# A hybrid gMLP and retention layer on eight cores: two small transposing DMAs per retention step, and four gate groups held in PSUM

## The reference, cut to what matters

```
q = rotary(r_q);  k = rotary(r_k)                 # 8 heads, 128 wide
ret = retention(q, k, r_v)                        # per head, chunk by chunk of 128 tokens:
#   scores = (q k^T * decay);  out = scores v + (q R) * cross_decay
#   R = R * chunk_decay + (k * w)^T v             # the state, carried to the next chunk
#   out = standardize(out)                        # over the 256 values of a head
yb = (ret * silu(r_z)) @ w_ob                     # the gate, then a projection
out = (sigmoid(g_a + b) * ya + sigmoid(g_b + b) * yb) @ w_out
x = layer_norm(ALPHA * x + out)
```

## Time and profile before

| | us |
|---|---|
| median of three runs | 2732.95 (2732.89 to 2733.12) |
| the profiled execution, its own time | 2732.09 |
| its span on the slowest core (core 2) | 2730.5 |
| span of the even cores | 2728.6 to 2730.5 |
| span of the odd cores | 2684.2 to 2694.5 |
| PE busy / PEld / DVE / ACT / POOL on core 2 | 2697.4 / 1420.4 / 1108.5 / 643.5 / 194.5 |

### The profile page before, as it was taken

One profiled execution on the slowest core, in us unless ns is written; L12 is line 12 of the kernel. 1 busy time (PEld: TensorE's weight loads), 2 busy tenths in 40 slices (PEclk: granted clock), 3 DMA queues, 4 the chain that ended last, 5 costly groups with the idle time before them and its releaser, 6 DMA issues.

```text
span 2730.5 us, 42159 instructions; the slowest of 8 cores (2684.2 to 2730.5 us)
## 1 busy us (share of the span) xinstructions
PE 2697.4 (99%) x15129; PEld 1420.4 (52%) x15170; DVE 1108.5 (41%) x2686; ACT 643.5 (24%) x1546; POOL 194.5 (7%) x370
## 2 busy tenths in 40 slices
PE   8999999999999999999999999999999999999998
PEld 6556666555555666666544444444555444444443
DVE  1444441166664422222474343411666642122157
ACT  1221110155554111111001211111555621111100
POOL 2000000000000000000001000000000000000000
PEclk9999999999999999999999999999999999999999
DMA  9843444333225433344649464444333544444443
GB/s 159 175 78 63 69 74 71 60 63 58 47 53 109 70 73 68 69 70 70 143 174 214 81 93 72 73 87 76 63 63 63 108 78 89 74 70 86 77 122 134
DMA packets 62420, 241.54 MB, mean 88 GB/s; under 512 B 7424, under 2 KB 7552, under 8 KB 58624
## 3 DMA queue, kind: packets, MB, share of 16 engines
q0 software_dynamic: 52560, 193.49, 41.3%
q1 hardware_dynamic: 9648, 45.27, 4.6%
HBM read 413.31 MB, written 18.87 MB: 158 GB/s over the span
## 4 chain that ended last, share of the span: by engine, by line
PE 97%; DMA 1%; ACT 1%; issue 0%; DVE 0%; POOL 0%; POOLq 0%; DVEq 0%; ACTq 0%
PE ps_all L236 96%; PE ps_all L245 1%; DMA ring<-w 1%; ACT L257 0%; DVE xy_85 L264 0%; ACT aT L257 0%; POOL xT L292 0%; POOL ring L292 0%; POOLq L988 0%; ACT zth_124 L257 0%; DVE stv L282 0%; ACT rs_66 L257 0%; ACT rs_63 L257 0%; ACT rs_65 L257 0%; ACT zth_123 L257 0%
## 5 line engine op out<-in xcount | busy, mean ns | idle before, releaser
L236 PE MATMUL ps_all<-xT,ring 128*128 128x384 bf16 (+1 forms) x6400 | 1206.6, 348 | 0.8 <-ACT rs_65 L257 0.7
L236 PEld LDWEIGHTS ps_all<-xT,ring 128*128 128x128 bf16 x6400 | 622.1, 98 | 536.6 <-issue 2.4
L236 PE MATMUL ps_all<-ring,xT 128*128 128x512 bf16 (+1 forms) x3744 | 731.1, 353 | 5.1 <-DMA xT<-xT 3.1
L236 PEld LDWEIGHTS ps_all<-ring,xT 128*128 128x128 bf16 x3744 | 337.4, 98 | 341.1 <-issue 6.9
L236 PE MATMUL ps_all<-aT,ring 128*128 128x384 bf16 (+1 forms) x2520 | 481.2, 347 | 2.1
L236 PEld LDWEIGHTS ps_all<-aT,ring 128*128 128x128 bf16 x2560 | 250.2, 98 | 220.0
L292 POOL DMA_DIRECT2D ring<-w x352 | 187.7, 541 | 2409.9 <-PE ps_all L236 2013.4
L236 PE MATMUL ps_all<-ring,yT 128*128 128x512 bf16 x1088 | 235.2, 379 | 0.0
L236 PEld LDWEIGHTS ps_all<-ring,yT 128*128 128x128 bf16 x1088 | 106.4, 98 | 128.4
L275 DVE CAST yT<-ps_all 128x384 bf16<-128x384 f32 (+1 forms) x40 | 24.5, 611 | 205.7 <-PE ps_all L236 205.7
L264 DVE SCALAR_TENSOR_TENSOR ogb_129<-ogb_129,ps_all 128x384 f32<-128x384 f32 (+1 forms) x40 | 24.3, 608 | 183.6 <-PE ps_all L236 183.6
(11 more groups left out here) (271 smaller groups left out, 1895.4 us busy)
## 6 DMA issues: line engine op xcount, KB each, us to landing
ring<-w POOLq DMA_DIRECT2D x352, 512.0 KB, 6.3
xy_86<-x SPq DMA_DIRECT2D x9, 1024.0 KB, 6.8
out<-xy_86 SPq DMA_DIRECT2D x18, 512.0 KB, 3.1
xy_85<-x SPq DMA_DIRECT2D x8, 1024.0 KB, 5.4
out<-xy_85 SPq DMA_DIRECT2D x16, 512.0 KB, 2.6
xT<-xT POOLq DMA_DIRECT2D x9, 512.0 KB, 26.3
xT<-xT POOLq DMA_DIRECT2D x4, 1024.0 KB, 21.3
bias_71<-bias_s SPq DMA_DIRECT2D x2, 1024.0 KB, 12.2
```

The source lines that it names most:

```text
L236: return self.S.op("pe", lambda e: e.matmul(out, lhsT=l, rhs=r, start=start, stop=stop), [l, r], [out])
```

## The change: what it does

The two PE transposes of `ybp` and ACT's copy of their result go. In their place, right after the norm of a step has been written to `ybp`, SP issues two transposing DMAs of 128 x 128 bf16 each, from `ybp` straight into `aT`, with one key per half and buffer (eight keys). The state product moves from bank 4 to bank 7. Behind the loop, four gate groups instead of seven carry the rest of the retention steps (i = N to N+3); their results stay in banks 0 to 3 while the steps run; then comes one more `small_post`, and then the four tanh and their products. All later groups are gated at once, and take the banks in turn from bank 4. The area for the temporary buffers is 2 KB per partition larger, and the gate's and the prefix state's buffers begin 2 KB later in it.

```
+    def dma_tr(self, key, out, in_):
+        self.S.op("sp", lambda e: e.dma_start_transpose(out=out, in_=in_), [in_], [out], key=key)
...
         def small_pe(i):
-            a, b_, c_, y = i - 2, i - 3, i - 4, i - 7
+            a, b_, c_ = i - 2, i - 3, i - 4
...
-                    self.mm(self.bank(4)[:, 128:384], m.qkt[c_ % 6][:, 1, :], m.v[c_ % 6][:], True, True)
+                    self.mm(self.bank(7)[:, 0:256], m.qkt[c_ % 6][:, 1, :], m.v[c_ % 6][:], True, True)
...
-            if 0 <= y < N:
-                for j in range(2):
-                    self.tr(self.bank16(7)[:, j * 128:(j + 1) * 128], m.ybp[y % 4][:, j * 128:(j + 1) * 128])
...
         def small_post(i):
...
-                    self.stt(m.U[:, h, :], m.U[:, h, :], float(self.gC[h]), self.bank(4)[:, 128:384], ALU.mult, ALU.add)
+                    self.stt(m.U[:, h, :], m.U[:, h, :], float(self.gC[h]), self.bank(7)[:, 0:256], ALU.mult, ALU.add)
...
             if 0 <= z < N:
+                h, c = divmod(z, n)
                 self.act(m.ybp[z % 4][:], self.bank(5 + z % 2)[:, 0:256], AF.Identity, scale=r[:, 0:1], bias=r[:, 1:2])
-            if 0 <= y < N:
-                h, c = divmod(y, n)
-                self.act(self.aT[:, 2 * h:2 * h + 2, c * 128:(c + 1) * 128],
-                         self.bank16(7)[:, 0:256].rearrange("p (j t) -> p j t", j=2), AF.Copy)
+                for j in range(2):
+                    self.dma_tr("ty%d%d" % (j, z % 4), self.aT[:, 2 * h + j, c * 128:(c + 1) * 128], m.ybp[z % 4][:, j * 128:(j + 1) * 128])
...
+        def gate(ct, c0, k, b):
+            tk = slice(c0 * CH, (c0 + k) * CH)
+            ps = self.bank(b)[:, 0:k * CH]
+            th = m.zth[self.rot("zt", 4)][:, 0:k * CH]
+            self.act(th, ps, AF.Tanh, scale=0.5)
+            self.stt(th, th, 1.0, ps, ALU.add, ALU.mult)
+            a = self.aT[:, ct, tk]
+            self.stt(a, a, 0.5, th, ALU.mult, ALU.mult)
+
         i = N
-        step = 0
+        held = []
+        self.nbank = 4
         for ct in range(16):
             s = self.w_take(1)
             for (c0, k) in self.sp:
-                tk = slice(c0 * CH, (c0 + k) * CH)
-                drain = i < N + 7
-                b = step % 3 if step < 7 + 3 else self.next_bank()
-                step += 1
-                ps = self.bank(b)[:, 0:k * CH]
-                self.group(ps, [(m.ring[:, s, kt, :], self.xm(kt, c0, k)) for kt in range(KT)])
-                if drain:
+                b = i - N if i < N + 4 else self.next_bank()
+                self.group(self.bank(b)[:, 0:k * CH], [(m.ring[:, s, kt, :], self.xm(kt, c0, k)) for kt in range(KT)])
+                if i < N + 4:
+                    held.append((ct, c0, k, b))
                     small_pe(i)
                     small_post(i)
                     i += 1
-                th = m.zth[self.rot("zt", 4)][:, 0:k * CH]
-                self.act(th, ps, AF.Tanh, scale=0.5)
-                self.stt(th, th, 1.0, ps, ALU.add, ALU.mult)
-                a = self.aT[:, ct, tk]
-                self.stt(a, a, 0.5, th, ALU.mult, ALU.mult)
+                    if i == N + 4:
+                        small_post(i)
+                        for g in held:
+                            gate(*g)
+                else:
+                    gate(ct, c0, k, b)
             self.w_free()
```

More of the change, by code:

```diff
@@ L674, in small_pe @@
                 self.mm(ob, m.qkT[c_ % 4][:, 0, :], m.Rg[c_ % 3][:], False, True)
-            if 0 <= y < N:
-                for j in range(2):
-                    self.tr(self.bank16(7)[:, j * 128:(j + 1) * 128], m.ybp[y % 4][:, j * 128:(j + 1) * 128])
         def small_post(i):
-            a, b_, c_, y = i - 2, i - 3, i - 4, i - 7
-            z = i - 5
+            a, b_, c_, z = i - 2, i - 3, i - 4, i - 5
             if 0 <= z < N:
@@ L873, in plan_memory @@
     s0 = top[0]
-    top[0] += 32768
+    top[0] += 34816
     assert top[0] <= nc.sbuf_usable_end, (top[0], nc.sbuf_usable_end)
@@ L885, in sub @@
             pos[0] += (size + 31) // 32 * 32
-            assert pos[0] <= s0 + 32768
+            assert pos[0] <= s0 + 34816
             return at(name, shape, dt, off)
@@ L916, in plan_memory @@
     m.cs = a("cs", [128, NMAX, 128], F32)
-    assert a.pos[0] <= s0 + 24576
-    a = area(24576)
+    assert a.pos[0] <= s0 + 26624
+    a = area(26624)
     m.zth = [a("zth%d" % i, [128, 512], F32) for i in range(4)]
-    a = area(24576)
+    a = area(26624)
     m.yh = [a("yh%d" % i, [128, KT, 128], BF16) for i in range(2)]
```

## The result

The changed kernel takes 2712.03 us, against 2733.03 for the kernel before on the same chip: a ratio of 0.9922, 95% interval 0.9900 to 0.9945. Times are medians of all executions; ratios, and ranges of single executions (2711.18 to 2712.23 here), leave out those that ran slower at a lower clock on one die or both, which would move a median by 0.3 us at most, in e5 by 2.5. The gain is 21.0 us; 25.8 were forecast.

What follows compares the result with a forecast made beforehand. The prediction took PE, 97% of the slowest core's chain, as the bound. Its terms 13.3 + 9.5 + 3.0 = 25.8 us gave 2707 us; the forecast's own range was 2703 to 2712, the whole range 2702 to 2722.

Steps and rivals of the forecast that it cites:

- one term that was put at nothing: Waiting caused by the transposing DMAs that replace the PE transposes: forecast to add zero to the time.
- The two PE transposes: Retention loop: removing them saves PE 0.11 us per step over 122 steps, 13.3 us after one not gained.
- The drain: Last retention steps among the first gate groups: held gates gain 9.5 us in the first tile, 3.0 in the second.
- Is anything late next? ... Cost: nothing: Drain: bank 0 is free at 835.5, wanted at 840.7, 5 us to spare, so no new wait.
- The two DMAs: Per retention step, issued by SP: a pair gets through within 3.95 us, four buffers absorb lag; cost zero.
- I take zero: Cost forecast for the transposing DMAs; 5.38 us per pair was kept for the range.
- one pair of lag: Inside a weight burst at 5.38 us per pair, 2.7 pairs pass while 3.7 are made; four buffers cover it.
- The prediction's signs: Right: 3.95 us steps, seven groups in about 20 us, full clock, landing below 15 us. Wrong: ACT idle on DMAs.
- A: Rival: transposing DMAs set the loop's pace at 5.38 us per step, +149 us, 2882 us; chance 0.11.
- The mild form of A: Rival: DMA pair just above the loop step, 4.1 to 4.2 us paid in series, about 2731 us; chance 0.02.
- B: Rival: drain stays long as four held gates and last norms come in one lump, 2719.6; 0.07 together with C.
- C: Rival: loop step stays 4.06 us through the norm-DMA chain or DVE, only drain gains, 2720.5; 0.07 together with B.

Runs made afterwards that it cites:

- e5: Changed kernel with each transposing DMA cut in two, four of 64 x 128 per step; 2881.04 us, ratio 1.0527.
- e1: Changed kernel with eight ybp buffers and sixteen DMA keys instead of four and eight; 2706.29 us, ratio 0.9901.
- e2b: Changed kernel with the last head's weight refill moved later and made to wait for the tile's last transposing DMAs; 2707.32 us, ratio 0.9903.
- e7: Changed kernel with the transposing DMAs left out, so the normed output never reaches aT; 2707.0 us, ratio 0.9904.
- e6: Changed kernel with one transposing DMA of 128 x 256 per step instead of two of 128 x 128; 2712.34 us, ratio 0.9925.
- e2: Changed kernel with the weight refill put behind the drain in program order only, without a wait; 2710.38 us, ratio 0.9917.

## Why the prediction was right, and where it was not

The direction, the mechanism of both gains and the range held. The time lies at the upper end of the forecast's own range (2703 to 2712), 5 us above the 2707, and the reason is one term that was put at nothing. By its own steps:

**1. The two PE transposes: right.** 13.3 us forecast. Core 2 gained 818.16 - 810.73 = 7.43 in the first loop. From the first reader of `aT` to the second tile's first gate group it took 2159.74 - 959.53 = 1200.21 and takes 2140.53 - 946.76 = 1193.77, 6.44 less. Together 13.9. The 0.69 us in front of the second gate stayed (0.65), as the step said, though it did not grow.

**2. The drain: the second tile right (3.0 forecast and measured), the first tile mis-sized.** 9.5 us were forecast; the change gave 5.3 on core 2 and 1.7 on core 0. The layout itself was good: e1 runs the seven groups in 19.9 us, and one table load follows the last norm where they alternated before. What failed is the sentence "Is anything late next? ... Cost: nothing". It followed bank 0, which has time to spare, and passed over banks 5 and 6. The second and third group behind the held ones take these two, and the last two norms must have read them first. With the norms in time that costs nothing (e1); a late norm goes to PE there at once.

**3. The two DMAs: the pace right, the lag wrong, and this is the cause.** "I take zero" held in the loop: a pair takes SP 2.3 us of 3.95. It rested on one pair of lag "against four buffers", 15.8 us. The lag was too small even there: during a head's refill a DMA landed as late as 11.8 us (core 0, 700 to 795), three steps and not one, so the loop was covered with less to spare than forecast. And 15.8 us is the loop's reuse distance only. In the first tile's drain the change itself brings the steps closer, since a gate group lasts 2.60 us and a projection group 3.45, and the distance is 9.6 us (e1). At this very place the last head's four slots are refilled. There, on core 0, the DMA took 14.64 us, ACT's norm waited 6.89, PE 4.60, and the granted clock fell behind it. The term put at zero measures 137.88 - 131.70 = 6.2 us on core 0 and 136.03 - 131.70 = 4.3 on core 2. The second tile's groups last 3.45 us and its first steps keep 3.95; there one norm waits 1.78 us and PE does not, though its weights are refilled alike. The price taken from the earlier trace rows, 2.69 us per DMA one behind the other, was a wrong picture as well: issue costs 1.16 us each, and a DMA inside a burst is late by its landing, 14.64 us for the one that PE waited for, not by its spacing.

So the sum: 13.9 + 5.3 + 3.0 = 22.2 us on core 2, whose span fell from 2730.5 to 2708.3. Core 0, 0.9 us shorter before, is now longer by 2.3: its wait is the longer one, and its drain had less to gain (below). Where the wait is taken away the forecast's gain of 25.8 us is met, each against the kernel before on its chip: 27.0 (e1), 26.4 (e2b), 26.3 (e7).

The prediction's signs were the right ones to look for. Of those that would show it wrong, one appeared: idle time of ACT before a norm that ends with a DMA into `aT`. And of those that would show it right, three failed in the first tile's drain on core 0: the seven groups did not take about 20 us (the seventh began 832.00 - 809.94 = 22.1 us after the first), the granted clock did not stay full, and landing passed 15 us (19.4 at most).

**The rivals.** *A* did not happen with two DMAs per step and did with four (e5). The 1309 ns that the Trainium skill gives for a DMA transpose ("VectorE: DVE Perf Modes", The three transpose paths) made an estimated 2.6 us per pair; the rows show 2 x 1.16 = 2.3 to issue them, and e5 and e6 that this price is per DMA, not per size. Its advice for TensorE did not hold here: by the earlier trace rows against the loop above, two transposes cost PE's path 0.11 us per step and in the loop the DMAs cost it none. The mild form of A, each DMA paid behind the other, did not happen (e2b). The 2.0 us that the prediction takes for it from the Trainium skill ("DMA: Bandwidth & Descriptors", Anatomy of one DMA) is given in that section for DMAs that POOL issues; those of SP here landed after 2.2 us at best. *B* happened in part, from another side: it was not the lump of four tanh that kept the bank, but the norm behind the DMA. *C* did not happen.

Not settled: in the drain of before core 2 fell to a granted clock of 0.72, and so did core 6; core 0, with waits of the same kind, stayed at 1.00, as did core 4, and took 958.52 - 818.90 = 139.62 us. So some 1.75 of the 9.5 us were core 2's clock, and why two of four cores lost it was not tried. Nor why landing in the changed kernel goes up to 19 us on cores 0 and 6 and only to 14 on cores 2 and 4, or how much of that lateness the closer steps add to the refill.

## What to carry to other kernels

A buffer that a DMA reads must cover the longest landing, not the mean, and its cover in time is the number of buffers times the step at that place: where a change shortens the steps, work the cover out again there. Look for what else fills the DMA engines at that place; a load burst on an idle queue is moved by a wait, not by a later place in the program (e2 against e2b). Where waits go, follow every bank that the next groups take, not only those that the change holds.

## What the runs showed of the hardware

- Issuing a transposing DMA of bf16 costs SP 1.16 to 1.18 us in the median, whether it moves 64 x 128 (1.18, e5), 128 x 128 (1.16) or 128 x 256 (1.17, e6). Four per 3.95 us are too many.
- Its landing takes 2.2 us at best. While POOL's weight loads run it takes up to about 12 us in the loops and up to 19.4 in the first tile's drain, where the steps are closer (core 0); with the loads held back the median in the same 40 us is 2.3 (e2b) instead of 5.6 (e1). The Trainium skill ("Trainium Kernel Development and Optimization", Key Constraints) says that DMAs issued by SP and by POOL run on the same 16 engines and interleave; the trace agrees: a queue of its own did not keep the small DMAs from being late while the large loads ran.
- On core 0 a PE gap of 4.60 us ended at 832.00, and the window from 830 to 835 has a mean granted clock of 0.66, so it was partly at the level of 1.2 GHz; the window in front, from 825 to 830, with the larger part of the gap, was at 1.00, the level of 2.4 GHz. On core 2, behind a gap of 2.75 us, the clock from 828.3 to 831.0 was 0.50, the lower level. In e1 and e2b, without the gap, every window there is at 1.00.
